# Layer norms from column sums of the raw stream, and output chunks added to the stream straight from PSUM

## The reference

```python
for l in range(2):                      # first block
    h = x * (1 + scale[l]) + shift[l]
    y = mixer[l](h)                     # layer 0 gated MLP and pooling, layer 1 latent attention
    x = layer_norm(ALPHA * x + (1 + gate[l]) * y, ln_g[l], ln_b[l])
for l in range(2):                      # second block, "layers 2 and 3" of the kernel
    h = rms_norm(x, norm_g[l]) * (1 + scale[l]) + shift[l]
    x = x + gate[l] * hybrid[l](h)      # retention and stick-breaking attention
return rms_norm(x, final_g)
```

## Time and profile before

| | |
|---|---|
| runs (us) | 1420.35, 1421.29, 1426.9 |
| median (us) | 1421.29 |
| profiled execution, its own time (us) | 1423.26 |
| its span, first to last instruction (us) | 1421.5 |
| mean granted TensorE clock | 0.985 |
| PE / DVE / ACT / POOL busy, share of span | 95% / 63% / 41% / 22% |

### The profile page before, as it was taken

One profiled execution on the slowest core, in us unless ns is written; L12 is line 12 of the kernel. 1 busy time (PEld: TensorE's weight loads), 2 busy tenths in 40 slices (PEclk: granted clock), 3 DMA queues, 4 the chain that ended last, 5 costly groups with the idle time before them and its releaser, 6 DMA issues.

```text
span 1421.5 us, 17578 instructions
## 1 busy us (share of the span) xinstructions
PE 1353.4 (95%) x6875; PEld 1145.8 (81%) x6875; DVE 891.8 (63%) x1289; ACT 582.4 (41%) x883; POOL 317.6 (22%) x206
## 2 busy tenths in 40 slices
PE   2999999999999989999999999999999999999997
PEld 1988888678888878788888888878887788888876
DVE  6754544764684578887444776686666577675553
ACT  1423222322344255665322565543343466543341
POOL 0200200155410016554354200001114300011123
PEclk9999999999999999999999899999999999999998
DMA  9443334224333311121334033222313322211211
GB/s 374 162 163 133 134 137 148 114 101 151 113 133 134 111 67 53 49 79 45 133 134 163 30 142 111 90 89 89 118 60 133 133 90 66 83 60 60 78 42 59
DMA packets 30610, 155.14 MB, mean 109 GB/s; under 512 B 3392, under 2 KB 3520, under 8 KB 19264
## 3 DMA queue, kind: packets, MB, share of 16 engines
q1 hardware_dynamic: 30528, 154.03, 29.9%
HBM read 151.92 MB, written 2.10 MB: 108 GB/s over the span
## 4 chain that ended last, share of the span: by engine, by line
PE 81%; DVE 7%; issue 5%; ACT 4%; DMA 1%; SPq 1%; POOL 0%; DVEq 0%; ACTq 0%; POOLq 0%
PE bank L748 23%; PE bank L750 23%; PE bank L749 23%; PE bank L1077 1%; PE bank L856 1%; DMA w_raw<-wt 1%; DVE neg_max L1676 1%; ACT pT L1373 1%; PE bank L1161 1%; PE bank L1135 1%; PE bank L755 1%; PE bank L874 1%; PE bank L1137 1%; ACT p_even L1364 1%; PE bank L1036 1%
## 5 line engine op out<-in xcount | busy, mean ns | idle before, releaser
L748 PE MATMUL bank<-h_lo,w_hi 128*128 128x512 f32 x1008 | 399.1, 396 | 5.6 <-DVE h_lo L1932 3.1
L750 PE MATMUL bank<-h_hi,w_hi 128*128 128x512 f32 x1008 | 394.2, 391 | 0.0
L749 PE MATMUL bank<-h_hi,w_lo 128*128 128x512 f32 x1008 | 394.0, 391 | 0.0
L1473 DVE TENSOR_TENSOR w_lo<-w_raw,w_hi 128x2048 fp32r<-128x2048 f32 (+2 forms) x91 | 201.9, 2219 | 95.1 <-ACT w_hi L1206 94.8
L748 PEld LDWEIGHTS bank<-h_lo,w_hi 128*128 128x128 f32 x1008 | 190.4, 189 | 46.5 <-issue 4.5
L750 PEld LDWEIGHTS bank<-h_hi,w_hi 128*128 128x128 f32 x1008 | 190.2, 189 | 40.6
L749 PEld LDWEIGHTS bank<-h_hi,w_lo 128*128 128x128 f32 x1008 | 190.3, 189 | 38.4 <-issue 0.5
L1206 ACT ACTIVATE w_hi<-w_raw 128x2048 fp32r<-128x2048 f32 (+2 forms) x91 | 166.7, 1832 | 12.4 <-DMA w_raw<-wt 8.8
L1501 DVE SCALAR_TENSOR_TENSOR acc<-ada_raw,cond,acc 128x1024 f32<-128x1024 f32 x70 | 100.8, 1440 | 0.0
L1279 ACT ACTIVATE tmp<-bank 128x512 f32<-128x512 f32 x48 | 28.6, 596 | 140.7 <-PE bank L750 129.6
L1949 POOL TENSOR_SCALAR q_dup<-rot_y 128x512 fp32r<-128x512 f32 x8 | 11.9, 1492 | 318.2 <-DVE rot_y L1512 318.2
(11 more groups left out here) (291 smaller groups left out, 2693.0 us busy)
## 6 DMA issues: line engine op xcount, KB each, us to landing
w_raw<-wt SPq DMA_DIRECT2D x83, 1024.0 KB, 5.8
ada_raw<-adat SPq DMA_DIRECT2D x80, 512.0 KB, 3.7
ada_first<-adat SPq DMA_DIRECT2D x16, 512.0 KB, 10.6
w_raw<-wt SPq DMA_DIRECT2D x8, 640.0 KB, 4.8
spare_raw<-wt SPq DMA_DIRECT2D x3, 1024.0 KB, 5.8
x<-xt SPq DMA_DIRECT2D x4, 512.0 KB, 16.6
out<-outf SPq DMA_DIRECT2D x8, 256.0 KB, 2.2
poolw<-poolt SPq DMA_DIRECT2D x1, 1024.0 KB, 5.8
```

The source lines that it names most:

```text
L748: pe.matmul(dst, ah, bl, start=start, stop=False, skip_group_check=True)
L749: pe.matmul(dst, al, bh, start=False, stop=False, skip_group_check=True)
L750: return pe.matmul(dst, ah, bh, start=False, stop=stop, skip_group_check=True)
L1473: dve.tensor_tensor(w_lo[wb[T]][:, 0:n], w_raw[wb[T]][:, 0:n], f(w_hi[wb[T]][:, 0:n]), ALU.subtract).then_inc(w_lo_done, 1)
```

## The change

Output chunks of all four layers are no longer copied by ACT: DVE reads the bank and writes x = bank * gate + x in one instruction, and the bank is free at `post_done`. In layers 0 and 1 the gate is divided by ALPHA instead, and the layer norms' epsilon by ALPHA squared.

Of the sums over partitions, those of the finished slices move into the last OUT0 or OUT1 chunk, ahead of its product 12 of 16 (`partial_sums`); the last slice's sums stay behind the chunk (`last_sums`). For OUT1 five arrays are summed instead of two: the new three are x weighted by g squared and by g times b, and x squared weighted by g squared (g and b are layer 1's norm gain and bias). DVE builds the first two (`gain_parts`), ACT the weighted square, DVE adds it. From these sums the RMS norm of the layer norm's result is worked out in columns (`derived`), without forming the result first. A step `gain_sums` in layer 1 sums g and b terms once over the features.

At the border from layer 1 to 2, op `ln_h` replaces `ln` (l=2), the second statistics and `h`: DVE goes two slices ahead with the plain normalization, and multiplies by the second factor as soon as ACT has applied gain and bias. The piece of `ada_piece` of the last OUT1 tile moves behind that chunk's addition on DVE. `keep_busy` writes bank 3 instead of 4; 6 stand after the sums, none between the two broadcasts, 10 after the second.

```diff
@@ plan_steps
     for n in range(DC):
-        T = begin()
-        chunk("OUT1", T, n=n, l=1)
+        T = begin(late_ada=n == DC - 1)
+        chunk("OUT1", T, n=n, l=1, tmp=False)
         after_tile(T)
-    s = stat(D, 0, True, "sums", 7, (6, 5))
-    steps.append(dict(op="stat_bcast", **s))
-    steps.append(dict(op="ln", l=2, s=s["stat"]))
...
+        if l == 2:
+            first_norm = stat(D, 0, True, "sums", 7, (6, 5))
+            s = stat(D, 1, False, "derived", 7, (4,))
+            steps.append(dict(op="stat_bcast", **first_norm))
+            steps.append(dict(op="stat_bcast", **s))
...
+        steps.append(dict(op="ln_h" if l == 2 else "h", l=l, s=s["stat"]))
@@ tensor
+            def partial_sums(l):
+                pe.wait_ge(sums_done, l + 1)
+                if l == 1:
+                    pe.wait_ge(gains_done, DC - 2)
+                for i, part in enumerate((sum2, sum1, by_gain, by_bias, sq_gain) if l == 1 else (sum2, sum1)):
+                    for b in range(NB):
+                        pe.matmul(bank[:, 7, NB * i + b:NB * i + b + 1], part[:, b * P:(b + 1) * P], ones[:, 0:1],
+                                  start=i == b == 0, stop=False, skip_group_check=True)
...
+                    if d["n"] == DC - 1 and k == 12:
+                        partial_sums(d["l"])
...
-                    if d["width"] == D and d["stat"] < stats[-1]["stat"]:
+                    if d["width"] == D and d["stat"] not in (DERIVED - 1, stats[-1]["stat"]):
                         keep_busy(12 if d["mean"] else 10)
@@ scalar
+                if kind == "OUT1" and d["n"] < DC - 1:
+                    n = d["n"]
+                    act.wait_ge(post_done, d["post"])
+                    if n >= 2:
+                        act.wait_ge(gains_done, n - 1)
+                    act.activation(sq_part[:] if n else sq_gain[:], x[:, n, :], ACT.Square,
+                                   scale=col("ln_g", DC + n)).then_inc(sq_part_done, 1)
+                if direct[C]:
+                    return
...
+                elif op == "ln_h":
+                    l = d["l"]
+                    act.wait_ge(cols_done, l + 1)
+                    for k in range(DC + 1):
+                        if k < DC:
+                            act.wait_ge(ln_t, k + 1)
+                            act.activation(x[:, k, :], x[:, k, :], ACT.Identity, scale=col("ln_g", DC + k),
+                                           bias=col("ln_b", DC + k)).then_inc(x_new, 1)
+                        if k >= 1:
+                            act.wait_ge(h_t, H_T_BASE[op, l] + k)
+                            act.activation(h_hi[:, k - 1, :], tmp[:, (k - 1) % 2, :], ACT.Identity,
+                                           scale=h_scale[:, l, k - 1:k],
+                                           bias=h_shift[:, l, k - 1:k]).then_inc(h_hi_done, 1)
@@ vector
+            def gain_parts(n):
+                g, gb = gain_sq[:, n:n + 1], gain_bias[:, n:n + 1]
+                if n == 0:
+                    dve.tensor_scalar(by_gain[:], x[:, 0, :], g, None, ALU.mult)
+                    link(dve.tensor_scalar(by_bias[:], x[:, 0, :], gb, None, ALU.mult))
+                    return
+                if n >= 2:
+                    dve.wait_ge(gains_done, n - 1)
+                dve.scalar_tensor_tensor(by_gain[:], x[:, n, :], g, by_gain[:], ALU.mult, ALU.add)
+                link(dve.scalar_tensor_tensor(by_bias[:], x[:, n, :], gb, by_bias[:], ALU.mult, ALU.add))
+                dve.wait_ge(sq_part_done, n + 1)
+                dve.tensor_tensor(sq_gain[:], sq_gain[:], sq_part[:], ALU.add).then_inc(gains_done, 1)
...
-                    ins = dve.scalar_tensor_tensor(x[:, n, :], x[:, n, :], ALPHA, t, ALU.mult, ALU.add)
+                    ins = dve.scalar_tensor_tensor(x[:, n, :], bank[:, CHUNK_BANK[C], :], gate[:, l, n:n + 1],
+                                                   x[:, n, :], ALU.mult, ALU.add)
...
+                if d["lhs"] == "derived":
+                    dve.scalar_tensor_tensor(st_p[:], st_mean[:], gain_sum[:, 1:2], bank[:, 7, 3 * NB:4 * NB], ALU.mult,
+                                             ALU.add)
+                    link(dve.scalar_tensor_tensor(st_u[:], st_mean[:], gain_sum[:, 0:1], bank[:, 7, 2 * NB:3 * NB],
+                                                  ALU.mult, ALU.subtract))
...
+                    dve.tensor_scalar(st_var[:], st_q[:], w, gain_sum[:, 2:3], ALU.mult, ALU.max).then_inc(stv_done, 1)
+                    return
...
+                elif op == "ln_h":
+                    l, rho = d["l"], d["s"]
+
+                    def plain(k):
+                        link(dve.tensor_tensor(x[:, k, :], x[:, k, :], bank[:, 6, :], ALU.mult))
+                        dve.tensor_tensor(x[:, k, :], x[:, k, :], bank[:, 5, :], ALU.subtract).then_inc(ln_t, 1)
+
+                    dve.wait_ge(stb_done, rho)
+                    plain(0)
+                    derived_root(rho)
+                    plain(1)
+                    dve.wait_ge(stb_done, rho + 1)
+                    for k in range(DC + 1):
+                        if k < DC:
+                            dve.wait_ge(x_new, DC + k + 1)
+                            dve.tensor_tensor(tmp[:, k % 2, :], x[:, k, :], bank[:, 4, :], ALU.mult).then_inc(h_t, 1)
+                        if k + 2 < DC:
+                            plain(k + 2)
+                        if k >= 1:
+                            h_low(l, k - 1)
...
                 elif op == "stat_cols":
+                    if d["stat"] == DERIVED - 1:
+                        ada_piece(OUT1_FIRST["T"] + DC - 1 + 2 * SEC)
                     statistics(d)
+                    if d["lhs"] == "derived":
+                        h_columns(2)
+                        dve.memset(f(q_low[64:P, 0, :]), 0.0)
+                        dve.memset(f(q_low[0:64, 1, :]), 0.0)
```

More of the change, by code:

```diff
@@ L171, in plan_steps @@
         T = begin()
-        chunk("OUT0", T, n=n, l=0)
+        chunk("OUT0", T, n=n, l=0, tmp=False)
         after_tile(T)
@@ L201, in plan_steps @@
             steps.append(dict(op="kv_norm", s=skv["stat"]))
+        if i == 4:
+            steps.append(dict(op="gain_sums"))
         if i == 5:
@@ L647, in build @@
         stats = [d for d in steps if d["op"] == "stat_cols"]
+        DERIVED = next(d["stat"] for d in stats if d["lhs"] == "derived")
         RET_INDEX = {d["stat"]: i for i, d in enumerate(d for d in stats if d["lhs"] == "ret2")}
@@ L677, in build, with taken, wait_taken @@
             last_in[bk] = d["C"]
+        direct = [d["kind"][:3] == "OUT" for d in kinds]
+        post_at = {d["C"]: d["post"] for d in kinds}
+        def taken(C):
+            return C - sum(direct[:C])
+        def wait_taken(eng, C):
+            if C < 0:
+                return
+            if direct[C]:
+                eng.wait_ge(post_done, post_at[C])
+            else:
+                eng.wait_ge(chunk_taken, taken(C + 1))
+            if C in SPLIT_POST:
+                eng.wait_ge(post_done, SPLIT_POST[C])
         POST_VT_BEFORE = {}
@@ L754, in keep_busy @@
                 for i in range(n):
-                    pe.matmul(bank[:, 4, :], ident_r, rmats[:].rearrange("p a b -> p (a b)"), start=True, stop=True)
+                    pe.matmul(bank[:, 3, :], ident_r, rmats[:].rearrange("p a b -> p (a b)"), start=True, stop=True)
             h_seen = [0]
@@ L769, in chunk_pair @@
                 T, C = d["T"], d["C"]
-                pe.wait_ge(chunk_taken, C)
+                for c in range(2):
+                    wait_taken(pe, BEFORE_IN_BANK[C + c])
                 for k in range(DC):
@@ L796, in chunk_four, with last_sums @@
                         ins.then_inc(chunk_full, 1)
+            def partial_sums(l):
[6 more added lines that the diff above has]
+                                  start=i == b == 0, stop=False, skip_group_check=True)
+            def last_sums(l):
+                n = 3 if l == 1 else 1
+                weights = gain_cols[:, 0:n] if l == 1 else ones[:, 0:1]
+                pe.wait_ge(post_done, post_of["OUT%d" % l, l, DC - 1, 0])
+                for b in range(NB):
+                    pe.matmul(bank[:, 7, NB + b:NB * (n + 1):NB], x[:, DC - 1, b * P:(b + 1) * P], weights,
+                              start=False, stop=True, skip_group_check=True)
+                pe.wait_ge(last_sq, l + 1)
+                for b in range(NB):
+                    o = bank[:, 7, b:NB * 5:NB * 4] if l == 1 else bank[:, 7, b:b + 1]
+                    ins = pe.matmul(o, sqr[:, b * P:(b + 1) * P], weights[:, 0:2] if l == 1 else weights, start=False,
+                                    stop=True, skip_group_check=True)
+                return ins
             def out_chunk(d, ks):
@@ L1008, in _ @@
                     layer[0] = 1
+                elif op == "gain_sums":
+                    pe.wait_ge(gain_part_done, 1)
```

(19 more changed lines are left out.)

152 lines of the change are left out of this document (92 added, 60 removed).

## The result

The changed kernel takes **1415.2 us** (median of 8 runs, 1412.84 to 1418.81) beside 1422.39 (8 runs, 1420.35 to 1426.9) of the kernel before on the same chip: a ratio of 0.9947, interval 0.9931 to 0.9962. The gain is real, and its size sits on the half percent that I called the limit of one measurement: the interval reaches to both sides of it. The profiled execution took 1416.67, with a span of 1414.9 against 1421.5, 6.6 us less.

What follows compares the result with a forecast made beforehand. PE, busy 95% of the span, was taken as the bound. The terms gave -9.4 us at full clock and +5.3 for the clock, so -4.1: 1417.2 for the median, 1419.1 for the profiled execution, range 1411 to 1424.

Steps and rivals of the forecast that it cites:

- The new border: Layer 1 to 2, last OUT1 chunk full to first product: 30.2 us becomes 15.5 at full clock, 14.7 gained.
- The sums inside OUT1's chunk: Last OUT1 chunk: 20 one-column sums cost PE 4.5 us, waiting 0.4, half clock 2.5.
- The split that I named: DVE's split of weights, 2.48 us long, beside which POOL's sum took 3.22 instead of 1.29.
- the 2 us that I worked out from it for the wait: OUT1's last chunk: by the contention rule PE's wait would be 2.4 us in place of 0.4, 2 us more.
- Layer 0: Last OUT0 chunk: eight sums 1.8 us, wait 0.4, clock 0.8; behind it, copy saved 0.7, broadcast's clock loss 0.7.
- The hops: Borders behind OUT0, OUT2 and OUT3 each lose ACT's copy, 0.7 us: -2.1 in all.
- `gain_sums`: Adds one small matmul to PE's stream, 0.3 us at most.
- the first (the clock holds): Thin sums between dense products do not lower the clock: 1411.9 us; chance 0.27 for below 1414.2.
- The second (the clock takes more than the pass was worth): Last OUT1 chunk and layer 2's first products: seven half-clock spells give 1423.8 us, ten 1428.9; chance 0.14.
- The third (DVE's slices at 3.3): New border: DVE's factor waits for ACT, slices come at 3.3 instead of 2.6 us: 1420; chance 0.05.
- The clock takes about half of it back: Half-clock spells around the moved sums and the new border cost 5.3 us of the 9.4 gained at full clock.

Runs made afterwards that it cites:

- the second execution: The changed kernel run once more, unchanged, for another trace: 1414.11 us, a single execution.
- the combination: Changed kernel with OUT0's sums behind its chunk, OUT1's sixteen spread and four behind, h_lo earlier, ada piece back, columns and memsets earlier: 1409.03 us.

## Why the prediction was right

The median came 2.0 us below the forecast of 1417.2, and inside the range of 1411 to 1424; the profiled execution came 2.4 below the 1419.1 forecast for it. The gain itself was larger than forecast: 7.2 by the medians (the longer series of the kernel before has a median 1.1 above the one that I reckoned from), 6.6 and 8.7 by the spans of the two pairs of traces, where I had 4.1. A range that also holds "no change" is a weak test; the terms are a better one. By the prediction's own terms:

- **The new border.** Forecast 15.5 at full clock and 1.3 for the clock, 16.8; measured 16.70. The full-clock part was right: in the second execution, whose last sums ran at full clock, the first small step comes 2.79 behind the chunk (forecast 2.8), and though the first broadcast was slowed there too, the first plain slice 7.91 (7.8) and the first product 15.33 (15.5). The place of the clock's share was wrong. I put it on the fillers and the first products. It fell on the last slice's sums (784.76, 1.61 long) and the first broadcast: 788.95 to 792.32 is 3.4, where I took 2.1. So the first plain slice waits for the broadcast (9.28 behind the chunk; forecast 7.8) and not for DVE's columns and memsets, which end at 791.24. From there on the chain is 7.42 against 7.7 forecast.
- **The sums inside OUT1's chunk.** Forecast 4.5 for their length, 0.4 wait and 2.5 clock, 7.4; measured 6.10. The length was right: 4.56 in the run where the clock held. The wait wasn't there at all. The clock took the remaining 1.5, one stretch of 3.4 us at half speed and not one and a half. In the other three executions of the same chunk (18.21, 18.60, 18.62) it took 2.8 to 3.2, so 2.5 was a fair middle and the first trace a mild one.
- **Why no wait.** POOL's last sum ended at 771.92, two us ahead of the sums. I took it at 3.22 from the trace before; it took 1.63. Before, POOL's sum began at 768.85, with a split of weights already under way on DVE, which began at 767.79 and took 3.12. (The split that I named, at 765.39 and 2.48 long, was over by then.) Now the split starts only at 770.68, behind the new weighted sums and behind the start of POOL's sum. At OUT0, where nothing was put ahead of the splits, POOL's last sum still took 3.21, and PE waited 0.47. The Trainium skill's rule (SBUF — State Buffer, Who interferes with whom), by which a DVE instruction with two SBUF inputs contends with a GpSimd instruction that reads SBUF, agrees with these rows: beside POOL the second weighted sum took 1.79 and the addition 1.41, where the first weighted sum, which began just ahead of POOL's first sum, took 0.75 and POOL's sum 1.80 instead of 1.29. The direct addition, with one input in PSUM, took 0.75 in all 16 places. But the 2 us that I worked out from it for the wait did not come: the new operations took turns with POOL and pushed away a worse neighbour.
- **Layer 0.** Forecast 1.8, 0.4 and 0.8 in the chunk and nothing net behind it, 3.0; measured 2.56 and 0.47, 3.03. The wait is in the row, 0.47. That the sums agree so well is luck in part: the clock didn't fall in this chunk but behind it, and in the second execution the two are 2.55 and 2.11.
- **The hops.** Forecast -0.7 at OUT2; measured -0.68. Both traces have a fall of the clock in this border; in three of the other runs, which have none there, it takes 7.10 instead of 8.21, a cost that no term of the forecast names. At the end of the kernel forecast -0.7; measured -1.84. The rest is the clock: before, it had already fallen when the last broadcast ran (1.9 us), and now the broadcast, at 1.37, is for the most part ahead of the fall. In the second execution it is not (2.07 us), and this place gains 1.1.
- **`gain_sums`.** Forecast 0.3; it can't be told from the scatter of layer 1, 373.5 to 376.3 in the runs that have it.

So in the first trace the cost that was too large, 1.3 in the OUT1 chunk (0.4 wait, 0.9 clock), and the gain that was too small, 1.1 at the end, make the 2.4. Layers 2 and 3, which the forecast held unchanged, cancelled (-2.67 and +2.77) there by luck. In the second pair they don't: layer 2 again has 2.7 less, layer 3 only 0.3 more. No term of the forecast has these 2.7, the clock in a layer whose products stay the same. They alone would be most of the 3.1 that the medians gained beyond 4.1.

Of the rivals, the first (the clock holds) is refuted by 0.55 and 0.60 behind the sums; the run with the sums spread, in which it did hold in both chunks, took 1413, where I had given 1411.9 for a clock that holds throughout. The second (the clock takes more than the pass was worth) did not come. The rule named there, by which the low clock is the default and activity releases it (the Trainium skill, TensorE: Matmul & The Clock Gate, The HAM clock gate), agrees as to the place, behind thin work; the size was 10.2 us at half speed from 777 to 792, three such stretches and not seven. The third (DVE's slices at 3.3) did not either: from factor to factor DVE needs 1.9 to 2.5.

One more thing I had told too simply. The old pass was dear not for its work alone: its last five groups of sums ran at half clock, PE finishing at 798 the sums of slices that DVE had finished by 793. From 786 to 804 the kernel before had a granted clock of 0.62, 13.7 us at half speed, and 3.4 more at 778 to 782. The change takes out these 17.1 and has 10.2 us (777 to 792) in their place. Over the whole span the time at half speed, added up from the granted clock in each trace, is 42.4 before, 39.3 and 34.1 in the two executions after, and 29.1 in the combination. "The clock takes about half of it back" was right by place, but the kernel as a whole isn't slower clocked than it was.

## What to carry to other kernels

Thin matmuls that are moved off a border into a dense stream cost their own length there, plus what the clock does behind them: what the border can hide is better left there (the sums behind the chunk were the best single edit here, 1411.4), and what is moved is better put in twos to fours between full products. An operation that is shortened gains nothing while another engine's work fills the same gap; look at what else ends there (here the sums over the other slices hid ACT's copy at two of four borders). And when a gain of one to three us is to be shown, compare the stretch and not the total: a stretch at half clock somewhere else is as large.

## What the runs showed that I had not expected

- The kernel before draws its stretches at half clock at nearly the same places in both traces (447, 512, 778, 789, 990, 1062, 1109 us, within 0.5 of each other); the changed kernel, with equal instructions, doesn't: 1229 and 1362 in one, neither in the other.
- In the first trace the clock falls at the very end of the thin run: the window 776 to 778, in which PE did nothing but one-column matmuls, shows 1.00 and PE busy throughout; the next one, for the most part full products, 0.55. So most of what it costs is paid by dense work that comes after. (In two other traces it fell halfway through the run, at 776.7.)
- A neighbour's gain can come by a detour: POOL's sum went from 3.22 to 1.63 us although DVE got three more operations beside it, because those pushed the long split of weights out of its way.
